# Two token streams through a fp32 transformer step: at each normalisation, four weight pieces used stream by stream on both sides

## The chip, the cores and the metric

The kernel runs on one core of one Trainium2 chip. The metric is the device time of one execution in microseconds (us); lower is better. The core has a matrix engine (PE, called TensorE) with its own weight loads (PEld), a vector engine (DVE), a scalar engine (ACT), a general engine (POOL) and a queue engine (SP) that issues most of the transfers. Each takes its own instructions strictly in the order of the program; they wait for one another through semaphores.

## The reference, cut to what matters

Two streams of 128 tokens by 2048 channels (context tokens, stream 0; latent tokens, stream 1) go through two layers with the same weights, in float32:

```python
h = rms_norm(x, norm_mix_pre[l]) * (1 + cm) + sm           # cm, sm, gm, cf, sf, gf: modulation vectors
mix = attention_and_gmlp(h @ w_in[l])                      # w_in 2048 x 4608
x = x + gm * rms_norm(mix @ w_out[l], norm_mix_post[l])    # w_out 2048 x 2048
h = rms_norm(x, norm_ffn_pre[l]) * (1 + cf) + sf
f = (silu(h @ w_gate[l]) * (h @ w_up[l])) @ w_down[l]      # 5632 hidden channels
x = x + gf * rms_norm(f, norm_ffn_post[l])
```

The modulation vectors are `silu(cond) @ mod_w[l] + mod_b[l]`, six vectors of 2048 for each layer and stream. So between two weight matrices there stands twice in each layer the same bridge: square sums of the last product, a first reciprocal root, the new x, square sums of x, a second reciprocal root, the normalised x, its transposition, its scale and shift. Here each such bridge is called an edge. Edge 0 lies between w_out and w_gate of layer 0, edge 1 between w_down of layer 0 and w_in of layer 1, edge 2 is edge 0 of layer 1, and edge 3 is the end (only the first half of a bridge, then the output).

## The kernel before, in words

**Weights.** Every weight matrix is read in pieces of 256 rows by 512 columns (512 KB, `KB = 2` blocks of 128 rows). A float32 product is made of three products of shorter numbers: ACT copies a piece to a rounded form (`whi`, L1038), DVE subtracts to get the rest (`wlo`, L1268); this is `split`. For each block of 128 rows and each stream, `products` (L739) issues three matmuls, each with its own weight load: x low by whi, x high by wlo, x high by whi. One piece is thus 12 matmuls (2 blocks, 2 streams, 3 products), one unit of 8 pieces (`UNIT`) is 96 matmuls and fills 128 x 512 results of both streams, in the banks A0 and A1, or B0 and B1. `raw`, `whi` and `wlo` are rings of four pieces (`RING`), and ACT and DVE split four pieces ahead of PE (`LEAD`): piece j+4 can only be split when PE has used piece j (`w_used`). The transfer of a piece waits until its place in `raw` has been split (`lo_ready`).

**Order at an edge.** `dense` (L707) runs a unit, both streams in each piece. After the last unit of w_out or w_down ACT and DVE read the banks to `f`, square (`square`, L1052), gate (`gated`, L1437) and make the mean (`mean_square`, L1313), POOL raises it to the power -1/2 (`power`, L617), DVE makes the new x (`post`, L1427), ACT squares that, POOL makes the second root, DVE multiplies (`normal_chunks`, L1343), PE turns blocks of 4 x 128 columns of one stream (`turn_x`, L829), DVE and ACT scale and shift them (`pre_part`, L1353 and L1088), ACT rounds them (`high`, L1056) and DVE takes the rest (`low`, L1322). All of this is done for both streams at once, with one wait for both. PE may begin the next unit when the first block of both streams has passed (`xt_ready`); the second block comes at row block 4, and the turns of blocks 2 and 3 stand between the matmuls at row blocks 1 and 3. Two of the four pieces that lie ahead are split at the edge by ACT at once and by DVE one in each pause (`left_over`, `LEFT = 2`); the two others are split before it.

**Modulation.** The products for the modulation vectors are put between the pieces in bursts of four pieces of `mod_w` (`mod`, L801, 16 matmuls of 32 columns of weights); they have a ring of four pieces of their own (`mraw`). In the units of w_out there are four bursts, one after piece 3 of each unit, and two more follow behind the last unit, before the turns of edge 0 or 2, with the read-out of the finished vector (`mod_tail`: ACT L1067, PE L821, DVE `mod_cols`). Other vectors are made by DVE in the pieces of w_gate, w_up and w_down (`accumulate`, L1290), from the ninth piece after edge 0 and 2 on. At edge 1 nothing of them lies on PE before the first unit; w_in has a burst after piece 3 of a unit.

## Time and profile before

| | |
|---|---|
| time, median of 3 runs | 2475.52 us (2470.42 to 2483.92) |
| profiled execution, its own time | 2475.68 us |
| its span, first to last instruction | 2473.9 us |
| PE busy | 2323.5 us (94%), mean granted clock 0.97 |
| DVE busy, ACT busy, POOL busy | 1507.5 us (61%), 984.0 us (40%), 65.9 us (3%) |
| moved by DMA | 609.94 MB, mean 247 GB/s |

The span is what the trace covers; the profiled execution's own time holds 1.8 us more. PE's clock has two levels here, 2.4 GHz (granted clock 1.00) and 1.2 GHz (0.50).

### The profile page before, as it was taken

The numbers are of one execution on the slowest core, as the hardware profiler recorded it, in microseconds if no ns is written. First come the engines' busy times: TensorE is split into PE (matmuls) and PEld (weight loads), VectorE is DVE, ScalarE is ACT, GpSimd is POOL, SyncE is SP. The second block draws the span as 40 slices with busy tenths as digits, with TensorE's granted clock in tenths as the row PEclk, the third lists the DMA queues.
The fourth block names the chain that finished last, engine by engine and source line by source line (L and its number), as shares of the span: only waits on it lengthen the run. The fifth ranks groups of instructions, "written<-read, shape, count | busy, mean of one in ns | idle before, by whom it ended". The sixth has DMA issues, their size and how long they took to land.

```text
span 2473.9 us, 28233 instructions
## 1 busy us (share of the span) xinstructions
PE 2323.5 (94%) x10892; PEld 1810.9 (73%) x10892; DVE 1507.5 (61%) x1637; ACT 984.0 (40%) x1253; POOL 65.9 (3%) x90
## 2 busy tenths in 40 slices
PE   5999978989999999999979998798999999999997
PEld 2776646768888887888757775475888888878886
DVE  2555453568886788688765444545788644454455
ACT  2333242454444443334444333345444444434443
POOL 1001020000000000000000101000000000000000
PEclk8999989989999999999989999998999999999999
DMA  8779887758777777787746876776777666556664
GB/s 298 272 286 340 324 285 288 256 203 269 267 257 246 272 262 248 236 271 266 269 166 221 300 264 219 273 278 225 260 268 258 219 194 191 188 183 195 189 220 137
DMA packets 269318, 609.94 MB, mean 247 GB/s; under 512 B 19116, under 2 KB 19296, under 8 KB 267840
## 3 DMA queue, kind: packets, MB, share of 16 engines
q1 hardware_dynamic: 264832, 589.37, 70.0%
q0 software_dynamic: 4352, 18.76, 2.0%
q8 instruction: 87, 1.43, 0.2%
q14 instruction: 47, 0.39, 0.0%
HBM read 603.79 MB, written 5.45 MB: 246 GB/s over the span
## 4 chain that ended last, share of the span: by engine, by line
PE 85%; DMA 6%; issue 4%; DVE 2%; ACT 1%; SPq 1%; POOL 0%; POOLq 0%; DVEq 0%; ACTq 0%
PE bank_A L743 39%; PE bank_B L743 37%; DMA mraw<-in_mod_w 6%; PE bank_M L801 3%; PE bank_X L829 2%; PE bank_M L790 1%; PE bank_T L821 1%; DVE wlo L1268 0%; ACT xtmp L1088 0%; PE bank_M L733 0%; ACT junk L1052 0%; PE bank_B L915 0%; SPq L464 0%; ACT whi L1038 0%; DVE f L1343 0%
## 5 line engine op out<-in xcount | busy, mean ns | idle before, releaser
L1268 DVE TENSOR_TENSOR wlo<-raw,whi 128x1024 fp32r<-128x1024 f32 x736 | 898.9, 1224 | 794.5 <-ACT whi L1038 794.3
L1038 ACT CAST whi<-raw 128x1024 fp32r<-128x1024 f32 x736 | 770.2, 1049 | 1231.1 <-PE bank_A L743 622.5
L743 PE MATMUL bank_A<-whi,xt_lo 128*128 128x512 f32 x1136 | 450.3, 396 | 6.4 <-DVE xt_lo L1322 5.9
L743 PE MATMUL bank_A<-wlo,xt_hi 128*128 128x512 f32 x1136 | 446.1, 393 | 0.0
L743 PE MATMUL bank_A<-whi,xt_hi 128*128 128x512 f32 x1136 | 445.7, 392 | 0.0
L743 PE MATMUL bank_B<-whi,xt_lo 128*128 128x512 f32 x1104 | 433.6, 393 | 0.5 <-issue 0.5
L743 PE MATMUL bank_B<-wlo,xt_hi 128*128 128x512 f32 x1104 | 430.0, 390 | 0.0
L743 PE MATMUL bank_B<-whi,xt_hi 128*128 128x512 f32 x1104 | 429.8, 389 | 0.0
L1290 DVE SCALAR_TENSOR_TENSOR acc<-mraw,cond,acc 128x1024 f32<-128x1024 f32 x240 | 297.1, 1279 | 0.0
L743 PEld LDWEIGHTS bank_A<-whi,xt_lo 128*128 128x128 f32 x1136 | 215.8, 190 | 71.0 <-issue 25.0
L743 PEld LDWEIGHTS bank_B<-whi,xt_lo 128*128 128x128 f32 x1104 | 207.2, 188 | 58.3 <-issue 15.1
L743 PEld LDWEIGHTS bank_A<-whi,xt_hi 128*128 128x128 f32 x1136 | 215.4, 190 | 45.6
L743 PEld LDWEIGHTS bank_A<-wlo,xt_hi 128*128 128x128 f32 x1136 | 215.8, 190 | 43.7
L743 PEld LDWEIGHTS bank_B<-whi,xt_hi 128*128 128x128 f32 x1104 | 207.2, 188 | 43.5
L743 PEld LDWEIGHTS bank_B<-wlo,xt_hi 128*128 128x128 f32 x1104 | 207.4, 188 | 41.8
L801 PE MATMUL bank_M<-mraw,cond 128*32 128x512 f32 x768 | 109.8, 674 | 42.9 <-DMA mraw<-in_mod_w 42.8
L743 PE MATMUL bank_A<-whi,ht_lo 128*128 128x512 f32 x352 | 138.9, 394 | 0.0
L743 PE MATMUL bank_A<-wlo,ht_hi 128*128 128x512 f32 x352 | 137.7, 391 | 0.0
L743 PE MATMUL bank_A<-whi,ht_hi 128*128 128x512 f32 x352 | 137.5, 391 | 0.0
L743 PE MATMUL bank_B<-whi,ht_lo 128*128 128x512 f32 x352 | 137.3, 390 | 0.0
L743 PE MATMUL bank_B<-wlo,ht_hi 128*128 128x512 f32 x352 | 137.0, 389 | 0.0
L743 PE MATMUL bank_B<-whi,ht_hi 128*128 128x512 f32 x352 | 136.9, 389 | 0.0
(190 smaller groups left out, 1429.7 us busy)
## 6 DMA issues: line engine op xcount, KB each, us to landing
mraw<-in_mod_w SPq DMA_DIRECT2D x384, 512.0 KB, 5.7
raw<-in_w_gate SPq DMA_DIRECT2D x176, 512.0 KB, 3.7
raw<-in_w_up SPq DMA_DIRECT2D x176, 512.0 KB, 4.2
raw<-in_w_down SPq DMA_DIRECT2D x176, 512.0 KB, 4.6
raw<-in_w_in SPq DMA_DIRECT2D x144, 512.0 KB, 6.0
raw<-in_w_out SPq DMA_DIRECT2D x64, 512.0 KB, 5.1
gate_mix<-gate_rows POOLq DMA_DIRECT2D x4, 1024.0 KB, 6.5
gate_ffn<-gate_rows POOLq DMA_DIRECT2D x4, 1024.0 KB, 9.5
```

What stands on the lines that cost most here:

```text
L743: mm = pe.matmul(bank[f"{pair}{s}"][:], xs[:, k, t], ws_[:, slot, kb, :], start=(k == first and n == 0), stop=(k == (nk - 1 if last is Non ...
L790: mm = pe.matmul(bank["M"][g:g + 32, :], cond[:, 2 * k:2 * k + 32], mraw[:, j % RING, kb, :], start=(k < 4), stop=(k >= KD - 4))
L801: mm = pe.matmul(bank["M"][32 * c:32 * c + 32, :], cond[:, 2 * k:2 * k + 32], mraw[:, ring_piece(m, j + c // 2) % RING, c % 2, :], start=( ...
L821: mm = pe.matmul(bank["T"][:, w * t:w * t + w], mrow[:, t * P:(t + 1) * P], sel[:], start=True, stop=True)
L829: mm = pe.transpose(bank[b][:, n * P:(n + 1) * P], t, ident[:])
L1038: act.copy(whi[:, ph % RING], raw[:, ph % RING]).then_inc(hi_ready, 1)
L1268: dve.tensor_tensor(wlo[:, ph % RING], raw[:, ph % RING], whi[:, ph % RING].bitcast(F32), ALU.subtract).then_inc(lo_ready, 1)
L1290: ins = dve.scalar_tensor_tensor(out=acc[:, h, s, :], in0=w, scalar=c, in1=acc[:, h, s, :], op0=ALU.mult, op1=ALU.add)
```

## The change

On both sides of an edge four pieces (`APART`) are no longer used by both streams in each piece. PE runs stream 0 through all four, reports `half_done`, and then runs stream 1 through the same four; `w_used` is raised in stream 1's pass. The edge's work is split by stream and written out by hand as one `turnover` on ACT and one on DVE, POOL gets four powers at an edge in place of two, and the eight turns of blocks get an order of their own (`turn_order`, `TURN_AT`): stream 0's blocks 0 and 1 before its pass of four pieces, stream 1's blocks 0 and 1 within that pass, the other four in stream 1's pass and at piece 4. All four pieces ahead are now split within `turnover`. In w_out the bursts for the modulation stand after pieces 3, 8, 13, 19 and 24 of its 32 pieces (`OUT_MODS`), one stays behind the end; the transfers of all six are issued between the pieces (`OUT_FETCH`). At the end the output of stream 0 is issued first. The changed places, shortened:

```diff
+APART = 4
+
+def turn_order(l, which):
+    if l == which == 0:
+        return [(s, b) for b in range(ND) for s in range(2)]
+    return [(0, 0), (0, 1), (1, 0), (1, 1), (0, 2), (1, 2), (0, 3), (1, 3)]
+
+TURN_AT = {((0,), 5): (2, 3), ((1,), 1): (4,), ((1,), 3): (5,), ((1,), 6): (6,), ((0, 1), 8): (7,)}
+
+def scaled_by_act(l, which, i):
+    return i % 2 == 1 if l == which == 0 else i in (0, 2, 5, 7)
...
+OUT_MODS = {3: (0, range(0, 4)), 8: (0, range(4, 8)), 13: (1, range(0, 4)), 19: (1, range(4, 8)), 24: (2, range(0, 4))}
+OUT_FETCH = {4: (0, (0, 1)), 5: (0, (2, 3)), 11: (0, (4, 5)), 12: (0, (6, 7)), 16: (1, (0, 1)), 17: (1, (2, 3)),
+             22: (1, (4, 5)), 23: (1, (6, 7)), 27: (2, (0, 1)), 28: (2, (2, 3)), 31: (2, (4, 5, 6, 7))}
...
-                both(u + 1, w, CH, m, l, LOAD_SECOND)
-                for i in range(1, ND // 2):
-                    both(i * 2 + u, w, i * 2 * CH, i + m, l, LOAD_FIRST)
-                    both(i * 2 + (u + 1), w, i * 2 * CH + CH, i + m, l, LOAD_SECOND)
+                for q in range(LEAD, ND * UNIT):
+                    i, j = divmod(q, UNIT)
+                    both(u + i, w, i * CH, js=[j])
+                    if q in OUT_FETCH:
+                        mi, js = OUT_FETCH[q]
+                        mod_chunk(m + mi, l, js)
                 first_unit(plan.at[(l, "up", 0)][0], a["w_gate"][l], 0)
-                mod_chunk(m + MOD_OUT, l)
                 for g, (c0, n) in enumerate(GROUPS):
                     u, _, _ = plan.at[(l, "up", g)]
...
                     first_unit(plan.at[(l + 1, "win")][0], a["w_in"][l + 1], 0)
             sp.wait_ge(kv_stored, 16 * 4 * DEPTH)
-            for n in range(ND):
-                for s in range(2):
+            for s in range(2):
+                for n in range(ND):
                     c = slice(n * CH, (n + 1) * CH)
-                    sp.wait_ge(x_new, 16 * DEPTH - 8 + 2 * n + s + 1)
+                    sp.wait_ge(x_new, 16 * DEPTH - 8 + ND * s + n + 1)
...
+            def edge_powers(l, which):
+                k = 1 + 4 * edge_of(l, which)
+                if last_edge(l, which):
+                    for s in range(2):
+                        power(ms[:, s:s + 1], rstd[:, s:s + 1], ms_ready, k + s + 1, rstd_ready)
+                    return
+                for s in (0, 0, 1, 1):
+                    k += 1
+                    power(ms[:, s:s + 1], rstd[:, s:s + 1], ms_ready, k, rstd_ready)
+            power(ms[:], rstd[:], ms_ready, 1, rstd_ready)
...
-            def dense(u, pair, i, hi, lo, nk=KD, ph=0, ready=None, m=None, behind={}):
+            def dense(u, pair, i, hi, lo, nk=KD, ph=0, ready=None, m=None, behind={}, first=0, last=0):
 
 
 
                 free(pair + "0", i)
                 free(pair + "1", i)
-                for j in range(nk // KB):
-                    pe.wait_ge(lo_ready, u * UNIT + (ph + j + 1))
-                    slot = (ph + j) % RING
-                    for kb in range(KB):
-                        k = j * KB + kb
-                        if ready:
-                            ready(k)
-                        mm = products(pair, k, hi, lo, slot, kb, nk)
-                    mm.then_inc(w_used, 1)
-                    if j in behind:
-                        mod(m, behind[j])
-                    dve_vector(u * UNIT + ph + j)
+                n = nk // KB
+                for js in (range(first), range(first, n - last), range(n - last, n)):
+                    together = js.start == first and js.stop == n - last
+                    for streams in [(0, 1)] if together else [(0,), (1,)]:
+                        for j in js:
+                            if streams[0] == 0:
+                                pe.wait_ge(lo_ready, u * UNIT + (ph + j + 1))
+                            slot = (ph + j) % RING
+                            for kb in range(KB):
+                                k = j * KB + kb
+                                if ready:
+                                    ready(k, streams)
+                                mm = products(pair, k, hi, lo, slot, kb, nk, streams=streams)
+                            if streams[-1] == 0:
+                                if j == n - 1:
+                                    mm.then_inc(half_done, 1)
+                                continue
+                            mm.then_inc(w_used, 1)
+                            if j in behind:
+                                mod(m, behind[j])
...
-            def turn_x(l, which, b):
-                for s, (bk, i) in enumerate(plan.at[(l, "pre_uses", which)][b]):
-                    pe.wait_ge(xn_ready, 8 * (2 * l + which) + 2 * b + s + 1)
-                    turn(bk, i, [f[:, s, (4 * b + t) * P:(4 * b + t + 1) * P] for t in range(4)])
+            def turn_x(l, which, i):
+                s, b = turn_order(l, which)[i]
+                pe.wait_ge(xn_ready, 8 * edge_of(l, which) + i + 1)
+                turn(*plan.at[(l, "pre_uses", which)][i], [f[:, s, (4 * b + t) * P:(4 * b + t + 1) * P] for t in range(4)])
 
             def pre(l, which):
 
 
-                def ready(k):
-                    if k in (1, 3):
-                        turn_x(l, which, 2 + k // 2)
+                done = xt_count(l, which) - 8
+                def ready(k, streams):
+                    if (streams, k) in TURN_AT:
+                        for i in TURN_AT[(streams, k)]:
+                            turn_x(l, which, i)
                     if k % 4 == 0:
-                        pe.wait_ge(xt_ready, xt_count(l, which) - 8 + 2 * (k // 4 + 1))
+                        pe.wait_ge(xt_ready, done + {(0,): 1 + k // 4, (1,): 3 + k // 4, (0, 1): 2 + k // 2}[streams])
                 turn_x(l, which, 0)
                 turn_x(l, which, 1)
...
-                    mod_tail(i + m)
-                mod(m + MOD_OUT)
+                for i in range(ND):
+                    at = {q % UNIT: mj for q, mj in OUT_MODS.items() if q // UNIT == i}
+                    def burst(k, streams):
+                        if k % KB == 0 and k // KB - 1 in at:
+                            mi, js = at[k // KB - 1]
+                            mod(m + mi, js)
+                    dense(i + u, "AB"[i % 2], i // 2 + use["AB"[i % 2] + "0"], xt_hi, xt_lo, ready=burst,
+                          last=APART if i == ND - 1 else 0)
+                mod(m + MOD_OUT, range(UNIT // 2, UNIT))
                 mod_tail(m + MOD_OUT)
                 ready = pre(l, 1)
...
+            def turnover(l, which, u, ph, pieces, use, split, m=None):
+                def x_squares(s):
+                    for n in range(ND):
+                        act.wait_ge(x_new, 8 * edge_of(l, which) + ND * s + n + 1)
+                        square(x[:, s, n * CH:(n + 1) * CH], ssx[:, s, n:n + 1])
+                n = ND - 1
+                if which == 0:
+                    act.wait_ge(half_done, edge_of(l, which) + 1)
+                    act.copy(f[:, 0, n * CH:D], bank["B0"][:]).then_inc(freed["B0"], 1)
+                act.wait_ge(freed["B0"], use["B0"] + 3)
+                f_square(0, n)
+                if last_edge(l, which):
+                    act.wait_ge(freed["B1"], use["B1"] + 3)
+                    return f_square(1, n)
+                split(u, ph + pieces)
+                split(u, ph + pieces + 1)
+                x_squares(0)
+                act.wait_ge(freed["B1"], use["B1"] + 3)
+                f_square(1, n)
+                if m:
+                    mod_row(m)
+                split(u, ph + pieces + 2)
+                split(u, ph + pieces + 3)
+                l2, w2 = l + which, 1 - which
+                act.wait_ge(vec_ready, vec_count(l2, w2))
+                pre_scale(l2, w2, 0)
+                pre_high(l2, w2, 0)
+                x_squares(1)
+                pre_high(l2, w2, 1)
+                pre_scale(l2, w2, 2)
+                pre_high(l2, w2, 2)
+                pre_high(l2, w2, 3)
...
+            def turnover(l, which, u, ph, pieces, split, vectors=None):
+                now, end = edge_of(l, which), last_edge(l, which)
+                sq, rs = sq_count(l, which), 1 + 4 * now
+                c = slice((ND - 1) * CH, D)
+                def last_chunk(s):
+                    if which == s == 0:
+                        return
+                    if s == 0:
+                        dve.wait_ge(half_done, now + 1)
+                    else:
+                        dve.wait_ge(w_used, u * UNIT + ph + pieces)
+                    b = f"B{s}"
+                    if which:
+                        dve.tensor_tensor(f[:, s, c], f[:, s, c], bank[b][:], ALU.add).then_inc(freed[b], 1)
+                    else:
+                        dve.tensor_copy(f[:, s, c], bank[b][:]).then_inc(freed[b], 1)
+                def add(s):
+                    for n in range(ND):
+                        t = slice(n * CH, (n + 1) * CH)
+                        dve.scalar_tensor_tensor(out=x[:, s, t], in0=f[:, s, t], scalar=rstd[:, s:s + 1], in1=x[:, s, t],
+                                                 op0=ALU.mult, op1=ALU.add).then_inc(x_new, 1)
+                last_chunk(0)
+                gated(l, which, ND - 1, 0, sq + 7)
+                mean_square(ssq, sq + 7, slice(0, 1))
+                if vectors:
+                    vectors(0)
+                dve.wait_ge(rstd_ready, rs + 1)
+                add(0)
+                last_chunk(1)
+                if end:
+                    gated(l, which, ND - 1, 1, sq + 8)
+                    mean_square(ssq, sq + 8, slice(1, 2))
+                    dve.wait_ge(rstd_ready, rs + 2)
+                    return add(1)
+                split(u, ph + pieces)
+                mean_square(ssx, sq + 11, slice(0, 1))
+                gated(l, which, ND - 1, 1, sq + 12)
+                mean_square(ssq, sq + 12, slice(1, 2))
+                l2, w2 = l + which, 1 - which
+                dve.wait_ge(rstd_ready, rs + 2)
+                normal(l2, w2, 0, 1)
+                if vectors:
+                    vectors(1)
+                dve.wait_ge(vec_ready, vec_count(l2, w2))
+                dve.wait_ge(rstd_ready, rs + 3)
+                add(1)
+                pre_low(l2, w2, 0)
+                split(u, ph + pieces + 1)
+                pre_scale(l2, w2, 1)
+                mean_square(ssx, sq + 16, slice(1, 2))
+                pre_low(l2, w2, 1)
+                dve.wait_ge(rstd_ready, rs + 4)
+                normal(l2, w2, 2, 3)
+                split(u, ph + pieces + 2)
+                pre_scale(l2, w2, 3)
+                split(u, ph + pieces + 3)
+                pre_low(l2, w2, 2)
+                pre_low(l2, w2, 3)
+                normal(l2, w2, 4, 5, 6, 7)
```

## Rows read from the trace of the kernel before

**Rows 1.** The page, chain that ended last, by engine.

```profile
PE 85%; DMA 6%; issue 4%; DVE 2%; ACT 1%; SPq 1%; POOL 0%; POOLq 0%; DVEq 0%; ACTq 0%
```

**Rows 2.** Windows (length; PE, PEld, DVE, ACT, POOL busy; PEclk; DMA share; GB/s).

```profile
406.67:503.89 97.22, 97.22 (x456) 74.47 (x456) 42.45 (x39) 36.92 (x45) 0.00 (x0) 0.98 0.79 277
498.45:552.66 54.21, 44.39 (x193) 32.15 (x193) 35.99 (x64) 28.52 (x56) 2.33 (x2) 0.78 0.56 196
1271.59:1326.81 55.22, 38.37 (x169) 29.46 (x169) 35.92 (x63) 27.44 (x54) 2.31 (x2) 0.78 0.47 160
1694.76:1747.21 52.45, 42.05 (x193) 30.41 (x193) 35.91 (x64) 28.77 (x56) 2.33 (x2) 0.84 0.54 195
```

**Rows 3.** Timeline of PE at edge 0: start, us, what, idle before.

```profile
503.50 0.39 PE L743 MATMUL bank_B<-whi,xt_hi 128*128 128x512 f32 x1
...
515.57 1.87 PE L821 MATMUL bank_T<-rsel,mrow 128*128 128x8 f32 x8 [0.72 <-ACT mrow L1067]
...
524.25 0.77 PE L743 MATMUL bank_A<-whi,xt_lo 128*128 128x512 f32 x1 [0.75 <-DVE xt_lo L1322]
524.82 0.63 PE L743 MATMUL bank_A<-wlo,xt_hi 128*128 128x512 f32 x1
525.24 0.63 PE L743 MATMUL bank_A<-whi,xt_hi 128*128 128x512 f32 x1
...
533.93 1.03 PE L829 MATMUL bank_X<-ident,f 128*128 128x128 f32 x8
```

**Rows 4.** Timeline of DVE at edge 0.

```profile
505.30 1.51 DVE L1437 TENSOR_TENSOR f<-f,gate_mix 128x512 f32<-128x512 f32 x2 [0.68 <-ACT junk L1052]
...
507.12 1.23 DVE L1268 TENSOR_TENSOR wlo<-raw,whi 128x1024 fp32r<-128x1024 f32 x1
508.96 5.39 DVE L1427 SCALAR_TENSOR_TENSOR x<-f,rstd,x 128x512 f32<-128x512 f32 x8 [0.61 <-POOL rstd L617]
...
518.16 1.67 DVE L1343 TENSOR_SCALAR f<-x,rstd 128x512 f32<-128x512 f32 x4
519.93 1.36 DVE L1353 TENSOR_SCALAR xtmp<-bank_X,scal,shift 128x128 f32<-128x128 f32 x4
522.81 1.29 DVE L1322 TENSOR_TENSOR xt_lo<-xtmp,xt_hi 128x512 fp32r<-128x512 f32 x2 [1.52 <-ACT xt_hi L1056]
```

**Rows 5.** Timeline of ACT at edge 0.

```profile
509.74 0.63 ACT L1052 ACTIVATE junk<-x 128x512 f32<-128x512 f32 x1 [1.78 <-DVE x L1427]
...
510.56 0.63 ACT L1052 ACTIVATE junk<-x 128x512 f32<-128x512 f32 x1
```

**Rows 6.** Timeline of POOL, edge 0 and edge 3.

```profile
507.29 1.63 POOL L617 TENSOR_TENSOR rstd<-ms,minus_half 128x2 f32<-128x2 f32 x1 [115.00 <-DVE ms L1314]
...
2464.40 0.71 POOL L617 TENSOR_TENSOR rstd<-ms,minus_half 128x2 f32<-128x2 f32 x1 [68.61 <-DVE ms L1314]
```

**Rows 7.** Chain in order of time: the unit after edge 0's first.

```profile
552.66 21.76 PE bank_B L743 x96
```

**Rows 8.** Timeline of PE: the burst in w_out's last unit.

```profile
490.50 0.39 PE L743 MATMUL bank_B<-whi,xt_hi 128*128 128x512 f32 x1
...
492.67 0.50 PE L743 MATMUL bank_B<-whi,xt_lo 128*128 128x512 f32 x1
```

**Rows 9.** Timeline of PE: edge 1's first turn, edge 3's last matmul.

```profile
1291.26 1.97 PE L829 MATMUL bank_X<-ident,f 128*128 128x128 f32 x8 [14.23 <-DVE f L1343]
...
2460.38 0.39 PE L743 MATMUL bank_B<-whi,ht_hi 128*128 128x512 f32 x1
```

**Rows 10.** Timeline of DVE at edge 3.

```profile
2462.41 1.51 DVE L1437 TENSOR_TENSOR f<-f,gate_ffn 128x512 f32<-128x512 f32 x2 [0.24 <-ACT junk L1052]
2463.95 0.16 DVE L1313 TENSOR_REDUCE msum<-ssq 128x2 f32<-128x8 f32 x1
...
2465.14 5.39 DVE L1427 SCALAR_TENSOR_TENSOR x<-f,rstd,x 128x512 f32<-128x512 f32 x8 [0.83 <-POOL rstd L617]
```

**Rows 11.** Busy time by window: w_in of layer 0, most DMA.

```profile
206.00:230.00 24.00, 24.00 (x129) 17.38 (x128) 11.97 (x14) 6.77 (x7) 0.00 (x0) 1.00 0.95 355
```

More of the change, by code:

```diff
@@ L1101, in start, with pre_late @@
+            def pre_late(l, which, j):
+                if j < 2:
+                    pre_pair(l, which, 4 + 2 * j)
             def start():
```

254 lines of the change are left out of this document (123 added, 131 removed).

## The prediction

> **What bounds the kernel now.** I read the chain that ended last first, since it says which engine's work sets the end: PE has 85% of it [rows 1]. Then the busy time by window, to see where PE is not full. In w_out of layer 0 it is busy for 97.22 of 97.22 us [rows 2]. In the windows around the norms it is busy for 44.39 of 54.21, 38.37 of 55.22 and 42.05 of 52.45 us, with a mean granted clock of 0.78 to 0.84, so even part of the busy time there is at half speed [rows 2]. I set these windows to begin 5.44 us before the last matmul's end (four pieces of one stream: 24 matmuls of 21.76 / 96 = 0.227 us each [rows 7]) and to end with the first unit behind the edge. The zero of all times below is that beginning.
>
> The timeline says what PE waits for. At edge 0 the last matmul ends at 503.89, the first one of w_gate starts at 524.25, 20.4 us later, behind DVE's xt_lo [rows 3]. Between them lies one long chain over DVE, ACT and POOL that works on both streams before it hands anything on: eight adds take 5.39 us, ACT's squares of x follow at 0.82 us each [rows 4, 5]. Edge 1 has 14.23 us without any PE work before its first turn [rows 9], edge 3 ends in the same chain's first half [rows 10]. The dense units themselves (21.76 us) the change leaves as they are: the same matmuls, the same pieces, so it can win only at the four edges. A perfect cover is bounded by these windows: 54.2 - 5.4 - 21.8 = 27.0 us for edge 0, of which turns and bursts need some 7.
>
> **The first matmul behind edge 0, after the change.** Stream 0 ends at 0, stream 1's pass covers PE until 5.4. DVE can gate stream 0 at 1.4, as it does now after both (503.89 to 505.30 [rows 3, 4]). One gate 0.7 (half of the two), then mean, root and hand-over 1.2, from edge 3, where nothing stands beside POOL (2463.95 to 2465.14 [rows 10]): the add starts at 3.3. Four adds, half of 5.39 [rows 4], to 6.0. DVE's copy of B1 0.7 and one split 1.2 [rows 4] to 7.9. ACT's squares begin 0.8 behind the add and take 0.82 each [rows 5]: 4.1 to 7.4, the last square of f to 8.2. DVE: mean 0.36, gate 0.7, mean 0.36, to 9.4 (POOL begins 0.45 behind a mean's start, 2463.95 to 2464.40 [rows 6, 10]; I count 0.36 on DVE); two normalised chunks at 0.42 (1.67 for four [rows 4]) to 10.3. Meanwhile the finished modulation vector: ACT's copy behind its squares to 8.8, PE's turn 1.87 [rows 3] to 10.8, DVE's four small instructions for the vectors, each like a mean's 0.16 with its hand-over [rows 10], to 11.5. Four adds for stream 1, 2.7, one low 0.65 (half of 1.29 [rows 4]): PE starts at 14.9. Before it was 524.25 - 498.45 = 25.8. That is 10.9 us earlier, but not yet the gain.
>
> **What is late next.** The weights. Formerly two pieces were split before the edge and two in its pauses; now all four can be split only as stream 1's pass frees them, and on DVE three of them stand behind the new x of stream 1. Between PE's start and piece 2 DVE has a split 1.2, a scale 1.36, a mean 0.36, a low 0.65, two normalised chunks 0.84, a split 1.2 [rows 4]: 5.6 us and about 0.4 of waits, so piece 2 is there at 21.0, where 12 matmuls of stream 0 take 2.7 us at full clock and 5.1 at half. Then the two turns of stream 1 (0.52 each at full clock: 1.03 for two [rows 3]), at half clock double, and behind them on DVE a scale 1.36 and the last split 1.2: piece 3 at 25.3. Its six matmuls end at 26.6. Stream 1's pass takes 5.4 and has three turns, 1.6, and one wait for a bank, 0.6: 34.2. A turn 0.5, four pieces for both streams 10.9, one late split 0.6: the unit ends at 46.2, before at 54.2. Edge 0 wins 8.0.
>
> **Waits that are new, and what queues behind them.** ACT waits for half_done with the last pieces' splits already behind it; what follows is the whole turnover, and nothing of it could start earlier. DVE's wait for the modulation vector (0.4 us by the chain above: it would be free at 10.3 and PE's turn ends at 10.8) holds the adds of stream 1, the split of piece 1 and thereby PE. ACT's copy of that vector stands behind eight squares, so each 0.1 us more there goes through to PE. SP has no new kind of wait, but the last four mod_w transfers are issued at piece 31 and need the burst after piece 24; behind them are the four first pieces of w_gate, which PE wants only at 14.9, over 20 us later. Those cost nothing.
>
> **Edge 2** is the same chain, but before it took only 52.45 (the clock rose earlier): 6.3. **Edge 1** has no modulation vector to wait for, has an add in place of the copy on the path (0.2 more), and one burst in its unit before and after: start at 14.3, end at 46.9 against 55.2: 8.3. **Edge 3:** gate at 1.6, as 2460.77 to 2462.41 [rows 9, 10], 0.7, 1.2, adds to 6.2; stream 1's last chunk 0.7, square 0.8, gate 0.7, mean and root 1.2, adds 2.7: 12.5 with hand-overs. The adds now end at 2470.53, which is 15.2: it wins 2.7, and the output transfers behind them stay as long.
>
> **The bursts.** Of the two that stood behind w_out's end, one is now before stream 0's last pass. There it costs 492.67 - 490.50 less one matmul, 1.94 us [rows 8], in each layer: before, both lay in the chain's shadow. That is -1.9 at edges 0 and 2. The two powers more at an edge lie on POOL, whose queue holds nothing else there. The weights of stream 0 and 1 in another order are the same number of weight loads and matmuls: nothing. The start of layer 0 keeps its order: nothing.
>
> **Sum.** 8.0 - 1.9 + 8.3 + 6.3 - 1.9 + 2.7 = 21.5 us. I take 3.0 off, 1 us for each of three edges, for the clock. The mean of 0.78 says that some 24 us of the windows of edges 0 and 1 ran at half speed, 0.84 some 17 us at edge 2 [rows 2]; my chain counts half speed only from PE's first wait to 20. Bounds of this term: nothing, or 4.4 us an edge, if it stays at 1.2 GHz until 32 (some 18 matmuls more and six turns; one matmul takes 0.43, 524.82 to 525.24, instead of 0.227 [rows 3, 7]). The profiled execution took 2475.68 us, 1.8 more than its span and 0.2 from the median: 2475.7 - 18.5 = 2457.
>
> **POOL beside DVE.** The first root took 1.63 us at edge 0, beside a split of 1.23 that began 0.17 earlier, and 0.71 at edge 3 beside nothing [rows 4, 6]. In the new order nothing follows the first mean on DVE, so I take 0.71; the second to fourth have a gate, a normalised chunk or a low beside them. If all were like the slow one it would be 3 x 0.9 more for an edge, 8 us in all. The Trainium skill (SBUF — State Buffer, "Who interferes with whom") says that a VectorE instruction with two SBUF inputs and a GpSimd one that reads SBUF shut each other out for a whole instruction, whichever began first. By that rule the trace agrees, and the second and third root would each add up to 0.9.
>
> **Rivals.** (a) *The clock stays down.* In the new order PE has four waits (2.1, 2 to 3, 1 and 2 us) where it had long ones, and thin work between them. The price is the upper bound above: 3 x 4.4 less the 3.0 taken, 2467. The Trainium skill (TensorE: Matmul & The Clock Gate, "HAM oscillation — how this bites in real kernels") tells of waits between short bursts of matmuls that keep the clock at half rate; by it this would be the likelier case, while the trace has the next unit at 21.76 us, full speed [rows 7]. (b) *DVE is the bound, so the split stays late.* If pieces 4 and 5 come 3 us late as well (DVE has 2 x (1.2 + 1.36 + 1.3) = 7.7 us of work for them, with its waits 9.8, covered by 10.9), 9 us of the gain go: 2466. (c) *The wait only changes its name:* every hand-over between the four engines is a place for some tenths more; 30 of them an edge at 0.2 us are 6, for three edges the whole 18: 2475. (d) *Better:* the clock never falls at edges 0 and 2 and no split is late: 3 + 3 x 2 more, 2448. (e) *Slower:* the bursts' transfers. From piece 4 to 31 of w_out there are now 28 + 24 transfers of 0.524 MB, 27.3 MB, in 27 x 2.72 + 5 x 1.94 = 83 us: 328 GB/s, where the window moved 277 [rows 2]. For it: that is 18% more than the stage ever had. Against: w_in moved 355 GB/s for 24 us with PE busy throughout [rows 11]. Were 277 all that this mix of rows gets, the stage would take 98.6 us, 15.5 more in each layer: 2457 + 31 = 2488. It decides the sign below 27.3 MB / 92.3 us = 296 GB/s.
>
> **How the numbers follow.** The sum, 2451 to 2463: 0.50. Better: 0.10. (a) and (b) together, 2463 to 2471: 0.22. (c): 0.10. (e): 0.08. Half a per cent, 12.4 us, is about what a measurement of this kernel can tell from no change: the limits are 2463.1 and 2487.9. Faster: 0.50 + 0.10 and a little of (a), 0.63; same: the rest of (a) and (b), 0.19, (c), and 0.03 of (e), whose price lies on the limit, 0.32; slower 0.05. The range leaves out (c), (e) and the far end of (d): 2448 to 2471.
>
> **What would show it.** Right: at edges 0 and 2 the first matmul on w_gate starts 9 to 11 us nearer to the end of w_out's last one (20.4 now, 9 to 10 then), PE then waits for wlo of pieces 2 and 3 and not for xt_lo, and w_out takes 2 us more. The last adds end in two groups of four. Wrong: waits of PE for mraw or of ACT for raw within w_out (e); a granted clock of 0.5 until the second unit (a); DVE without a pause of over 0.5 us until the ninth piece, and waits for wlo behind piece 4 (b).

## The result, and the profile after

The changed kernel takes 2453.68 us (median of 5 runs, 2450.63 to 2467.93) against 2475.52 (median of 5 as well); the ratio is 0.9925, 95% interval 0.9898 to 0.9952. Predicted were 2457.0 us, 2448 to 2471; the time lies below the 2463.1 from which the prediction calls a kernel faster. Its profiled execution has the highest time of the five (2467.93 us), only 7.8 us below the one of before (2475.68). A second measurement of the same kernel below (2457.73, ratio 0.9924) has a profiled execution near its median.

The page of the changed kernel, the chain that ended last, then PE's rows of the grouped instructions; before it was 85% PE, 6% DMA and 4% issue [rows 1]. PE's idle time ahead of the group shown was 6.4 us before and is 20.8 now: before, PE waited earlier, ahead of the turns ([rows 9]), now it waits for the operand itself.

```profile
PE 87%; DMA 5%; DVE 4%; ACT 2%; issue 1%; POOL 0%; SPq 0%; DVEq 0%; POOLq 0%; ACTq 0%
...
L793 PE MATMUL bank_A<-whi,xt_lo 128*128 128x512 f32 x1136 | 455.0, 401 | 20.8 <-DVE xt_lo L1419 12.8
```

Busy time by window: w_out of layer 0 up to the zero of edge 0 only (the first window of [rows 2] goes on to the last matmul's end, 5.44 us more; without them it was 91.78), its first 10 us and its last 33, then edges 0, 1 and 2 from their zero to the first matmul of the second unit behind them, as in [rows 2]:

```profile
408.84:503.07 94.23, 94.23 (x445) 70.85 (x442) 39.99 (x37) 34.81 (x43) 0.00 (x0) 0.98 0.87 300
408.84:418.84 10.00, 10.00 (x40) 8.17 (x37) 2.45 (x2) 2.10 (x2) 0.00 (x0) 0.81 0.97 346
...
470.00:503.07 33.07, 33.07 (x161) 24.58 (x160) 14.15 (x13) 11.30 (x15) 0.00 (x0) 1.00 0.92 327
...
503.07:549.72 46.65, 38.88 (x177) 29.41 (x176) 36.06 (x68) 29.73 (x57) 2.76 (x4) 0.89 0.40 123
1271.61:1319.92 48.31, 38.37 (x170) 29.03 (x169) 35.51 (x63) 28.61 (x55) 2.40 (x4) 0.86 0.52 166
1694.37:1741.07 46.70, 38.90 (x178) 29.40 (x176) 36.15 (x68) 29.74 (x57) 2.76 (x4) 0.89 0.39 125
```

At edge 0 PE is busy for 38.9 us instead of 44.4, since one of the two bursts has gone to w_out and more of the matmuls run at full clock, and idle for 7.8 instead of 9.8; both parts make the window shorter. Edge 1 shows another split: as many busy microseconds as before (38.4), but 9.9 idle for 16.9. In w_out PE has no idle time, and the last 33 us, with the transfers of the added pieces in them, move 327 GB/s.

Timeline of PE at edge 0 (zero 503.07), its main waits, and where its clock changed:

```profile
508.44 1.92 PE L853 MATMUL bank_M<-mraw,cond 128*32 128x512 f32 x16
511.54 1.06 PE L873 MATMUL bank_T<-rsel,mrow 128*128 128x8 f32 x8 [1.17 <-ACT mrow L1126]
512.72 1.09 PE L881 MATMUL bank_X<-ident,f 128*128 128x128 f32 x8
517.24 0.77 PE L793 MATMUL bank_A<-whi,xt_lo 128*128 128x512 f32 x1 [3.43 <-DVE xt_lo L1419]
...
522.87 0.50 PE L793 MATMUL bank_A<-whi,xt_lo 128*128 128x512 f32 x1 [0.49 <-DVE wlo L1368]
527.30 0.50 PE L793 MATMUL bank_A<-whi,xt_lo 128*128 128x512 f32 x1 [1.90 <-DVE wlo L1368]
...
528.88 0.63 PE L793 MATMUL bank_A<-whi,xt_lo 128*128 128x512 f32 x1
...
532.21 0.39 PE L793 MATMUL bank_A<-whi,xt_lo 128*128 128x512 f32 x1
```

The first matmul stands at 14.2 (25.8 before, [rows 3]). The next two waits are for `wlo`, the split weights of pieces 2 and 3. A matmul's duration of 0.63 instead of 0.39 is the mark of the lower clock. It stands in the matmuls from 517.24 to 521.6, and it comes back once, from 528.88 until 531.9, behind the 1.90 us of waiting. I call that the second fall.

Timeline of DVE at edge 0, what answers to [rows 4], and POOL, which answers to [rows 6]:

```profile
504.49 0.69 DVE L1593 TENSOR_TENSOR f<-f,gate_mix 128x512 f32<-128x512 f32 x1 [4.46 <-ACT junk L1111]
...
506.24 2.74 DVE L1481 SCALAR_TENSOR_TENSOR x<-f,rstd,x 128x512 f32<-128x512 f32 x4 [0.68 <-POOL rstd L651]
508.90 0.69 DVE L1476 COPY f<-bank_B 128x512 f32<-128x512 f32 x1
509.50 1.22 DVE L1368 TENSOR_TENSOR wlo<-raw,whi 128x1024 fp32r<-128x1024 f32 x1
...
512.98 0.18 DVE L1409 COPY modt<-bank_T 128x32 f32<-128x32 f32 x1
...
513.75 2.74 DVE L1481 SCALAR_TENSOR_TENSOR x<-f,rstd,x 128x512 f32<-128x512 f32 x4
516.41 0.69 DVE L1419 TENSOR_TENSOR xt_lo<-xtmp,xt_hi 128x512 fp32r<-128x512 f32 x1
...
521.60 1.22 DVE L1368 TENSOR_TENSOR wlo<-raw,whi 128x1024 fp32r<-128x1024 f32 x1
524.75 1.37 DVE L1449 TENSOR_SCALAR xtmp<-bank_X,scal,shift 128x128 f32<-128x128 f32 x4 [1.93 <-PE bank_X L881]
526.03 1.22 DVE L1368 TENSOR_TENSOR wlo<-raw,whi 128x1024 fp32r<-128x1024 f32 x1
```

```profile
505.64 0.56 POOL L651 TENSOR_TENSOR rstd<-ms,minus_half 128x1 f32<-128x1 f32 x1 [110.36 <-DVE ms L1414]
```

Here the last wait explains itself: DVE stands still for 1.93 us until PE has turned stream 1's block, with piece 3's split, which could have run (ACT had made its `whi` by 513.4), queued behind that scale. PE then waits 1.90 us for just this split.

The last adds, at edge 3 (zero 2451.18), come in two groups of four and end at 11.9; they ended at 15.2 before [rows 10]:

```profile
2454.52 2.74 DVE L1481 SCALAR_TENSOR_TENSOR x<-f,rstd,x 128x512 f32<-128x512 f32 x4 [0.68 <-POOL rstd L651]
...
2460.39 2.74 DVE L1481 SCALAR_TENSOR_TENSOR x<-f,rstd,x 128x512 f32<-128x512 f32 x4 [0.67 <-POOL rstd L651]
```

**All edges and kernels on one scale.** I read these from the timelines, in us behind each edge's zero (5.44 before the last matmul's end). "Unit end" is the first matmul of the second unit; for before that is 0.16 less than in [rows 2], which went by the chain. w_out is from its first matmul to the zero.

| kernel | edge 0: first matmul / unit end | edge 1 | edge 2 | edge 3: span's end | w_out, layer 0 / 1 |
|---|---|---|---|---|---|
| before | 25.80 / 54.05 | 25.22 / 55.06 | 26.03 / 52.29 | 18.57 | 91.78 / 90.38 |
| changed | 14.17 / 46.65 | 14.12 / 48.31 | 14.17 / 46.70 | 14.92 | 94.23 / 94.26 |
| changed, again | 14.15 / 45.04 | 14.11 / 46.68 | 14.15 / 46.69 | 14.92 | 92.50 / 93.92 |
| bursts only | 25.28 / 54.09 | 25.22 / 55.36 | 25.28 / 51.52 | 18.54 | 93.30 / 93.82 |
| bursts as before | 23.48 / 55.96 | 14.11 / 48.29 | 23.20 / 54.08 | 14.90 | 92.47 / 90.38 |
| apart ahead only | 23.59 / 49.65 | 23.54 / 50.87 | 23.75 / 49.00 | 14.92 | 94.73 / 92.50 |
| apart behind only | 20.08 / 50.96 | 19.55 / 53.70 | 20.07 / 50.97 | 20.33 | 94.42 / 92.50 |
| split beside the root | 15.06 / 47.59 | 15.06 / 47.63 | 15.05 / 47.51 | 14.93 | 94.47 / 93.78 |
| piece 3 before the scale | 14.16 / 43.88 | 14.11 / 45.49 | 14.16 / 43.84 | 14.93 | 93.15 / 92.52 |
| piece 2 earlier too | 14.16 / 42.68 | 14.12 / 44.59 | 14.16 / 43.44 | 14.89 | 93.43 / 92.72 |

**Where the time came from.** From the profiled execution of before to that of the changed kernel the edges give 7.4 + 6.8 + 5.6 + 3.7 = 23.4 us, w_out takes 2.4 + 3.9 = 6.3 back: 17.1. The spans differ by 7.8 only. The other 9.3 lie in stretches between the edges, whose code the diff leaves as it is nearly everywhere: 2.2 ahead of w_out of layer 0 (whose beginning scatters from 403.1 to 410.7 us over the executions here), 2.8 from the end of edge 0's unit to edge 1, 2.5 in w_in and the attention of layer 1, 1.8 behind edge 2. The second measurement's execution does not show the last three (+0.5, -0.6 and +0.4 us), so I take them for the profiled execution's own. In that second execution the edges give 26.6, w_out takes 4.3 back, w_out of layer 0 begins 4.1 later and the rest loses 0.2: 18.1, as its span (2455.8) has it.

### The profile page after: what moved, and what is told of

Read it like the earlier page. It is cut to its first block, busy times and chain, and to the rows that moved or that the text cites. A ratio compares the mean times of both kernels' runs of the same rounds, so it can differ in the third digit from the quotient of the medians.

```text
span 2466.1 us, 28259 instructions
## 1 busy us (share of the span) xinstructions
PE 2332.2 (95%) x10892; PEld 1816.3 (74%) x10892; DVE 1507.0 (61%) x1651; ACT 984.2 (40%) x1253; POOL 67.5 (3%) x97
## 4 chain that ended last, share of the span: by engine, by line
PE 87%; DMA 5%; DVE 4%; ACT 2%; issue 1%; POOL 0%; SPq 0%; DVEq 0%; POOLq 0%; ACTq 0%
PE bank_A L793 40%; PE bank_B L793 38%; DMA mraw<-in_mod_w 5%; PE bank_M L853 3%; PE bank_X L881 2%; PE bank_M L842 1%; DVE wlo L1368 1%; DVE x L1481 0%; PE bank_T L873 0%; ACT whi L1097 0%; DVE xtmp L1449 0%; PE bank_M L783 0%; PE bank_B L970 0%; ACT junk L1111 0%; PE bank_A L970 0%
## 5 line engine op out<-in xcount | busy, mean ns | idle before, releaser
L793 PE MATMUL bank_A<-whi,xt_lo 128*128 128x512 f32 x1136 | 455.0, 401 | 20.8 <-DVE xt_lo L1419 12.8
```

The lines of the kernel that those rows point to most:

```text
L793: mm = pe.matmul(bank[f"{pair}{s}"][:], xs[:, k, t], ws_[:, slot, kb, :], start=(k == first and n == 0), stop=(k == (nk - 1 if last is Non ...
```

## The experiments

The kernels were timed in two groups of four, on two chips, each group with its own runs of the kernel before (medians 2475.50 and 2475.11 us, 23 runs each). The changed kernel again, bursts only, bursts as before and piece 3 before the scale are the first group; across the groups, times are compared by the ratios.

**The same kernel again, and its halves: the bursts.** The first is the changed kernel unaltered.

> The changed kernel once more, with a profile, since its profiled execution (2467.93 us) was the slowest of five (median 2453.68). Theory (the gain is made in the four edges): the windows from stream 0's end to the first unit's end are 46.8, 48.5 and 46.8 us again within 0.5, whatever the whole time is, and the end takes 14.9; the spread of 17 us lies in the attention and at the start, where PE waits for mod_w. Rival (the edges themselves vary by several us from run to run, by the clock): an edge differs by over 2 us from the first trace.

It took 2457.73 us (2455.52 to 2458.87), ratio 0.9924 (0.9911 to 0.9937): the gain is 19 us with a narrower interval. Neither expectation holds: edges 0 and 1 end 1.6 us earlier each and edge 2 as before, which is more than 0.5 and less than 2. Of the 10.3 us between the two profiled spans 3.2 lie there, 2.1 in w_out and 6.9 in the stretches between; the start is 1.9 longer in the second. The clock did not fall a second time at edge 0 here (nor at edge 1), though the wait for piece 3 was again 1.90:

```profile
517.38 0.77 PE L793 MATMUL bank_A<-whi,xt_lo 128*128 128x512 f32 x1 [2.55 <-DVE xt_lo L1419]
523.01 0.50 PE L793 MATMUL bank_A<-whi,xt_lo 128*128 128x512 f32 x1 [0.17 <-DVE wlo L1368]
...
527.44 0.50 PE L793 MATMUL bank_A<-whi,xt_lo 128*128 128x512 f32 x1 [1.90 <-DVE wlo L1368]
529.62 0.60 PE L881 MATMUL bank_X<-ident,f 128*128 128x128 f32 x4
```

The kept traces price the second fall. From the first matmul to the unit's end there are 32.5 us with it and 30.9 without it at edges 0 and 2, and 34.2 and 32.6 at edge 1: 1.6 us each time. Over the five profiled executions in which PE waits 1.89 or 1.90 us for piece 3 (changed, again, bursts as before, apart behind only, split beside the root) it came at 9 of 15 edges. How long the first stretch at the lower clock lasts changes nothing: it ends 2.7 to 5.6 us behind the first matmul, and those times stay, since PE then waits for piece 2 or 3 anyway.

Two kernels then part the bursts from the reordering. "Bursts only" is the kernel before with the changed kernel's places for bursts and their transfers; "bursts as before" is the changed kernel with the old ones:

```diff
# bursts as before (from the changed kernel)
-                for q in range(LEAD, ND * UNIT):
-                    ...
-                    if q in OUT_FETCH:
+                both_rest(u, w, 0, m, l)
+                both(u + 1, w, CH, m, l, LOAD_SECOND)
...
                 first_unit(plan.at[(l, "up", 0)][0], a["w_gate"][l], 0)
+                mod_chunk(m + MOD_OUT, l)
...
-                    dense(i + u, ..., ready=burst, last=...)
-                mod(m + MOD_OUT, range(UNIT // 2, UNIT))
+                    dense(i + u, ..., m=i // 2 + m, behind=IN_SECOND if i % 2 else IN_FIRST, last=...)
+                mod(m + MOD_OUT)
```

> The kernel before with the new places of the modulation bursts and their transfers in w_out alone; the edges as before. Theory: w_out 1.94 us longer in each layer; at the edge the second burst no longer waits for its transfer, but the norm chain ends later anyway (T turn at 515.57 and the normalised chunk at 518.16 in the kernel before), so nothing comes back: 2475.5 + 3.9 = 2479 us. Rival (the transfers are too dense, 328 GB/s): waits of PE for mraw or of ACT for raw in w_out, 10 to 30 us more. Second rival (the burst's waits were on the path of the edge): 2475 or less.

> The changed kernel with the bursts of w_out where they were before: two stand behind the last unit again, the second with its transfer issued only there. Theory: at edges 0 and 2 the finished vector is now what the new chain waits for: second burst done some 16.7 us after stream 0's end, first matmul on w_gate at 23 instead of 14.1, 9 us more for each of two edges, less 1.94 in w_out: 2454 + 14 = 2468 us; edge 1 unchanged at 48.5. Rival (the norm chain on DVE and ACT is what counts and hides the bursts): 2454 - 3.9 = 2450.

Bursts only: 2483.16 us (2472.89 to 2486.86), ratio 1.0018 (1.0005 to 1.0031), a small loss; the ratio gives 4.5 us, the two medians 7.7. The two w_out's are 1.5 and 3.4 us longer, and the first matmul comes only 0.5 and 0.75 earlier, since the vector alone was not what held PE there. Bursts as before: 2468.93 us (2461.91 to 2476.57), ratio 0.997 (0.9956 to 0.9984). Edge 1, which has no vector on its way, keeps its 14.11; at edges 0 and 2 PE starts at 23.5 and 23.2, and the units there end 1.9 and 1.8 us later than in the kernel before. All that this kernel gains it gains at edges 1 and 3. Timelines of PE and of DVE at edge 0 of that kernel say why:

```profile
510.72 1.93 PE L853 MATMUL bank_M<-mraw,cond 128*32 128x512 f32 x8 [4.38 <-DMA mraw<-in_mod_w]
513.69 1.93 PE L853 MATMUL bank_M<-mraw,cond 128*32 128x512 f32 x8 [1.04 <-DMA mraw<-in_mod_w]
516.35 1.88 PE L873 MATMUL bank_T<-rsel,mrow 128*128 128x8 f32 x8 [0.72 <-ACT mrow L1120]
522.53 0.77 PE L793 MATMUL bank_A<-whi,xt_lo 128*128 128x512 f32 x1 [2.51 <-DVE xt_lo L1413]
```

```profile
518.26 0.19 DVE L1403 COPY modt<-bank_T 128x32 f32<-128x32 f32 x1 [9.23 <-PE bank_T L873]
```

The modulation weights land late, the vector is turned at 17.3 behind the zero instead of 8.5, and DVE stands still for 9.23 us until it has it. The scale of stream 0's block needs the vector itself; stream 1's adds, which the hand-written order puts behind it, add little: DVE ends them 0.3 us after ACT has rounded stream 0's block. So the moved bursts lose 4.5 us alone (0.18%) and are worth 11 (2468.93 - 2457.73) together with the new order.

**The two halves of the reordering.**

```diff
# apart ahead only
-TURN_AT = {((0,), 5): (2, 3), ((1,), 1): (4,), ((1,), 3): (5,), ((1,), 6): (6,), ((0, 1), 8): (7,)}
+TURN_AT = {((0, 1), 0): (2, 3), ((0, 1), 1): (4,), ((0, 1), 3): (5,), ((0, 1), 6): (6,), ((0, 1), 8): (7,)}
...
-                          first=APART if ready else 0)
# apart behind only
-                          last=APART if i == ND - 1 else 0)
...
-                        dve.wait_ge(half_done, now + 1)
+                        dve.wait_ge(w_used, u * UNIT + ph + pieces)
```

> The changed kernel, but only the last four pieces ahead of an edge are used by stream; the first unit behind it takes both streams together again, so PE needs stream 1's first block as well before its first matmul (its turns 2 and 3 go before piece 0). Theory (each half of the reordering gives PE 5.4 us of work on one side of the same chain, and the two lean on each other: the chain begins early because of the one, and PE can use the early stream 0 only because of the other): stream 0's adds still start at 3.3 behind the zero of the edge, but the first matmul only when stream 1's low part is there, at about 21 to 22.5, where the changed kernel has 14.2 and the kernel before 25.8; the unit ends at 49.5 to 51, not at 45 to 46.7; edge 3 keeps its 3.7. That is 3.5 us of gain at each of three edges and 3.7 at the last, less some 3 for the bursts: 2465 to 2469. Rival 1 (the gain is only the earlier start, the order behind the edge does nothing): 2457, as the changed kernel. Rival 2 (each half alone gives half): 2466 here and 2466 with the other half alone.

> The other half alone: both streams end together ahead of the edge, so stream 0's last chunk is complete only 5.44 us behind the zero; behind the edge the four pieces are used by stream, as in the changed kernel. Theory: the whole chain stands 5 us later: stream 0's adds start at 8.7 instead of 3.3, the first matmul comes at 19 to 19.6 instead of 14.2, the unit ends at 51 to 52 instead of 46.7, and edge 3 loses its 3.7 us and perhaps 1 more, since its adds come in two groups that nothing covers. Sum: 3 x 5 + 4 = 19 more than the changed kernel, 2474 to 2478, so next to nothing is left of the gain although half of the reordering is there. Rival 2 (each half alone gives half): 2466.

Ahead only: 2470.32 us (2463.17 to 2478.38), ratio 0.9979 (0.9964 to 0.9994). Behind only: 2477.46 (2473.34 to 2486.18), ratio 1.0009 (0.9999 to 1.0019), nothing. The unit ends are near those of the theory (49.0 to 50.9, and 51.0 to 53.7, of which edge 1's is 1.7 beyond it); the first matmul comes at 23.5 to 23.8 with the first kernel, 1 us and more beyond my 22.5, and at 19.6 to 20.1 with the second, up to 0.5 beyond. With the order ahead alone PE waits for stream 1's block; with the order behind alone the whole chain stands 5.4 to 5.9 later, and edge 3 ends 1.8 later than in the kernel before. PE's first turn and first matmul at edge 0, ahead only (zero 498.09):

```profile
516.55 1.94 PE L881 MATMUL bank_X<-ident,f 128*128 128x128 f32 x8 [7.72 <-DVE f L1434]
...
521.68 0.80 PE L793 MATMUL bank_A<-whi,xt_lo 128*128 128x512 f32 x1 [3.19 <-DVE xt_lo L1418]
```

Both rivals fall: it is not the earlier start alone, and neither half alone brings half of the time (5 us and -2 us by the medians, both together 18). But each of these three numbers has the cost of the moved bursts in it. At the edges alone, from the table, the order ahead gives 15.5 us, the order behind 4.0, both together 23.4 and 26.6 in the two executions. So the order ahead is the larger part, and what the two give only together is 4 to 7 us, with the second falls of 1.6 us in these numbers. What the edge's work split by stream gives without either order, no run tests.

**The root beside a split.**

```diff
                 if vectors:
                     vectors(0)
+                if not end:
+                    split(u, ph + pieces)
                 dve.wait_ge(rstd_ready, rs + 1)
                 add(0)
                 last_chunk(1)
...
-                split(u, ph + pieces)
```

> The changed kernel, but at the three inner edges DVE makes the first split of the next weights before it waits for the first root, where the kernel before had one, and no longer behind stream 0's adds. Theory (the root on POOL is drawn out by a split that runs beside it): the root takes 1.6 us as in the kernel before (1.63) and not the 0.56 of the changed kernel; stream 0's adds begin 1.1 later; of these 0.6 reach the first matmul, since the squares of x on ACT are what DVE's mean waits for and the split no longer stands before it: first matmul at 14.7 to 14.9 against 14.2, time 2457.7 + 3 x 0.6 = 2459.5. Rival (the 1.63 of the kernel before came from something else, the root takes 0.6 beside the split too): the adds begin 0.6 later, for the split itself, first matmul 14.2 to 14.4, time 2458.

Timelines of DVE and of POOL of that kernel at edge 0 (zero 499.65):

```profile
502.19 1.23 DVE L1368 TENSOR_TENSOR wlo<-raw,whi 128x1024 fp32r<-128x1024 f32 x1
503.87 2.74 DVE L1481 SCALAR_TENSOR_TENSOR x<-f,rstd,x 128x512 f32<-128x512 f32 x4 [0.46 <-POOL rstd L651]
```

```profile
502.22 1.62 POOL L651 TENSOR_TENSOR rstd<-ms,minus_half 128x1 f32<-128x1 f32 x1 [111.76 <-DVE ms L1414]
508.28 0.55 POOL L651 TENSOR_TENSOR rstd<-ms,minus_half 128x1 f32<-128x1 f32 x1 [4.44 <-DVE ms L1414]
```

The root is back at 1.62 (0.56 in the changed kernel), the adds begin at 4.2 instead of 3.2, and the first matmul at 15.06 instead of 14.17, 0.9 later where I expected 0.6. The time is 2460.98 us (2453.78 to 2467.1), ratio 0.9942 (0.9926 to 0.9958). The intervals of 0.9924 and 0.9942 touch, so that loss is shown by the first matmul at the three edges (0.9 each time), not by the time.

**The late weights.** The changed kernel has on DVE, behind stream 1's normalised chunks, the split of piece 2, the scale of stream 1's block, the split of piece 3. The scale waits for PE. Two kernels move splits ahead:

```diff
# piece 3 before the scale
                 split(u, ph + pieces + 2)
-                pre_scale(l2, w2, 3)
                 split(u, ph + pieces + 3)
+                pre_scale(l2, w2, 3)
# piece 2 earlier too
                 mean_square(ssx, sq + 16, slice(1, 2))
+                split(u, ph + pieces + 2)
                 pre_low(l2, w2, 1)
                 dve.wait_ge(rstd_ready, rs + 4)
                 normal(l2, w2, 2, 3)
-                split(u, ph + pieces + 2)
```

> The changed kernel with one exchange on DVE: the split of the fourth piece stands ahead of the scale of turn 3, in the 1.93 us in which DVE waits for that turn. Theory (the late weights are what is left of the edge): PE's wait of 1.90 us for wlo before piece 3 goes at each of three edges, and with it the fall of the clock behind it (0.43 for a matmul at 528.9 to 531.9, some 2 us): 2 to 4 us an edge, 2454 - 9 = 2445 to 2448 us. Rival (stream 1's inputs are next, the gain is lost again at once): PE waits for xt_lo before stream 1's pass, under 1 us an edge, 2452.

> As the kernel that splits piece 3 before it scales stream 1's second block (2449.96), and DVE splits piece 2 as well before the low part of stream 0's second block, 1.2 us earlier. Theory (with the splits of pieces 2 and 3 in time, what is left of the wait is stream 1's operand, whose chain the moved split delays by 0.4 to 0.8): the wait for wlo at piece 2, 1.1 us, goes and the one for xt_lo ahead of stream 1's pass grows from 0.5 to about 2; unit end 43.9 to 44.5, time 2450 to 2452, no gain. Rival (late weights are all that is left): 3 x 1.1 us less, unit end 42.8, time 2446.7.

The first took 2449.96 us (2447.5 to 2453.2), ratio 0.9898 (0.988 to 0.9915), where I expected 2445 to 2448. Its interval touches that of the changed kernel (0.9911 to 0.9937); the edges are clearer. Its unit ends come 1.2, 1.2 and 2.9 us before those of the changed kernel's second execution, and 2.8 to 2.9 before those of the first: 1.2 is the shorter wait (1.90 gone, 0.47 for `xt_lo` come in its place), 1.6 the second fall, which came at none of the six edges of these two kernels. The second took 2447.75 (2445.54 to 2449.41), ratio 0.9889 (0.9876 to 0.9902), the best of all, 1.2, 0.9 and 0.4 us before the first at the edges. PE at edge 0 in the first (zero 500.24) and in the second (zero 499.90):

```profile
520.02 0.50 PE L793 MATMUL bank_A<-whi,xt_lo 128*128 128x512 f32 x1 [1.11 <-DVE wlo L1368]
...
520.83 1.04 PE L881 MATMUL bank_X<-ident,f 128*128 128x128 f32 x8
...
524.40 0.50 PE L793 MATMUL bank_A<-whi,xt_lo 128*128 128x512 f32 x1 [0.47 <-DVE xt_lo L1419]
```

```profile
519.29 1.04 PE L881 MATMUL bank_X<-ident,f 128*128 128x128 f32 x8
522.86 0.51 PE L793 MATMUL bank_A<-whi,xt_lo 128*128 128x512 f32 x1 [0.45 <-DVE xt_lo L1419]
```

My theory for the second, that stream 1's operand would be the limit and nothing be gained, is wrong at the edges; the rival had the unit end at 42.8, and edge 0 has 42.68. The operand is no chain of its own: it begins with PE's turns of stream 1's blocks, and these stand in PE's queue behind piece 2. With piece 2 in time the turns come at 19.4 instead of 20.6, and the operand comes 1.2 us earlier too (23.0 for 24.2), so the wait for it stays 0.45. The times (intervals 0.988 to 0.9915 and 0.9876 to 0.9902) don't tell the two kernels apart by themselves.

## Why the prediction was right, step by step

| step | predicted | measured, changed kernel / again |
|---|---|---|
| edge 0: adds start / end | 3.3 / 6.0 | 3.2 / 5.9 |
| edge 0: first matmul | 14.9 | 14.2 / 14.2 |
| edge 0: piece 2, piece 3 ready | 21.0, 25.3 | 19.8, 24.2 / 19.8, 24.2 |
| edge 0: unit end without the clock term | 46.2 | 46.65 / 45.04 |
| edge 1: first matmul, unit end | 14.3, 46.9 | 14.1, 48.31 / 14.1, 46.68 |
| edge 2: gain | 6.3 | 5.6 / 5.6 |
| edge 3: gain | 2.7 | 3.65 / 3.65 |
| bursts, each layer | -1.9 | -2.4 and -3.9 / -0.7 and -3.5 |
| clock term, three edges | -3.0 | -4.8 / -1.6 (second falls, 1.6 each) |
| sum less the clock term | 18.5 | 17.1 / 22.4 in the stages; 0.75% (0.5 to 1.0) of the time, 18.6 |

**The chain ahead of the first matmul** was right link by link, 0.7 us too long. The vector came a little earlier than I took: its turn ran at full clock (1.06 us where I had 1.87 from [rows 3]); PE comes to it from a burst and 1.17 us of waiting, before it came from waits of 4.42, 0.82 and 0.72 us. So my wait of DVE for the vector (0.4) does not exist: at 512.98 DVE goes on without a stop. The distance from w_out's last matmul to w_gate's first is 8.7 us, just under the 9 to 10 that the prediction named as its sign.

**What is late next** was named rightly: PE's waits for `wlo` of pieces 2 and 3. The two kernels with the earlier splits show that this is a cost and not only a label: 6 and 9 us by the ratios.

**The clock term.** I took 3.0 off for three edges. Against the chain without it the unit ends lie 0.45, 1.4 and 0.55 us beyond (edge 2 against 52.45 - 6.3), 2.4 in all, in the first execution and 0.8 below it in the second. That is a net of two things. The second fall cost 1.6 us where it came: at all three edges of the first execution, 4.8, and at one of the second, 1.6. The rest of the chain was 2.4 too long in the prediction, the first matmul, taken up to 0.7 too late, among it. So 1 us for each edge is near the mean of the 15 places above (9 x 1.6 / 15), but no row had given it. The Trainium skill (TensorE: Matmul & The Clock Gate, "HAM oscillation — how this bites in real kernels") tells of waits between bursts of matmuls that send the clock down. By that section the trace agrees ahead of the first matmul, where PE waits 1.17 and 3.43 us between small pieces of work and the matmuls behind take 0.63. For the second fall there are only the rows: behind the same 1.90 us of waiting it came in some executions and not in others. Rival (a) had the clock low until 32 at each edge; in the changed kernel's two executions it was back by 19.8, and after a second fall by 28.9.

**The sum** was met more closely than its terms. The chain was 2.4 us too long at three edges and edge 3 gave 0.95 more; the bursts cost 2.5 more than taken in the first execution and 0.4 in the second; the second falls cost 4.8 and 1.6 where 3.0 were taken. The stages then give 17.1 and 22.4. That the ratio gives 18.6 where 18.5 was forecast is in part luck; the mechanism and the order of size are not.

**The bursts.** 1.94 was a good price for one burst: where w_out ran at full clock throughout, it took 92.50 in place of 90.38, 2.1 more. The rest of 3.9 is the lower clock in the first 10 us of the stage (0.81 in both layers of the first execution), which I had not counted, and which the kernel before shows too in its layer 0 (91.78). What the prediction missed is the other side of the step: it counted the bursts as a cost and took the early vector for granted in the chain. Without them the first matmul at edges 0 and 2 stays at 23, and nothing is won there.

**Edge 3** gave 0.95 more: the adds ended at 11.9 and not at 12.5, and the output behind them takes 0.4 less.

**POOL.** I took 0.71 for the undisturbed root and 0.56 came. The second root, where I feared up to 0.9 more, takes 1.10 at edges 0 and 2 and 0.54 at edge 1; the third takes 0.55, 0.75 and 0.55. At edge 0 this cost nothing: the second root ends at 512.15, and DVE works on its two means until 512.11. That a split was to blame for 1.63 is shown by putting one back (1.62).

**The rivals.** (b) is half true: pieces 2 and 3 were late, pieces 4 and on were not. (c), 0.2 us for each hand-over, would have shown in the first matmul; it came earlier than summed. (d) came by half at edges 0 and 1 of the second execution: no second fall, unit end 45.04 at edge 0, but the first matmuls still ran at 0.63 and piece 3 was still 1.90 us late; with the late splits removed as well it is 42.68. (e) is refuted: w_out moved 300 GB/s on average, above the 296 from which it would have decided the sign, and 327 in its last third, while PE was busy for 94.23 of 94.23 us. The longest wait for `mraw` in w_out over the kernels with the moved bursts is 1.1 us, once (split beside the root, layer 1). The kernel with the moved bursts alone loses 0.2%, not 1.3%.

What stays open is why the first profiled execution is slower outside the edges. The windows between them, in the first and in the second execution, behind edge 0 and then behind edge 1, say this much:

```profile
549.72:1271.61 721.89, 715.91 (x3212) 587.97 (x3211) 564.03 (x517) 297.94 (x321) 1.63 (x3) 0.99 0.78 257
1319.92:1600.11 280.19, 251.35 (x1315) 183.62 (x1313) 131.06 (x162) 99.29 (x147) 22.30 (x27) 0.96 0.77 267
```

```profile
548.27:1267.84 719.57, 713.59 (x3212) 586.09 (x3211) 563.49 (x517) 297.80 (x321) 1.63 (x3) 1.00 0.76 257
1314.52:1591.60 277.08, 249.92 (x1315) 182.81 (x1313) 131.33 (x162) 99.18 (x147) 22.17 (x27) 0.97 0.76 270
```

For the same number of matmuls PE is busy 2.3 and 1.4 us longer, at a granted clock lower by 0.01, and 1.5 us longer behind edge 2; that is 5.2 of the 6.9 us between the two executions in these stretches. What sent the clock down there no run shows.

## What to carry to other kernels

When a chain between two matrix products works on two independent streams, use the last weight pieces before it and the first ones behind it stream by stream: each half alone gave 5 us or nothing, both gave 18 to 22. And it needs everything else on the chain moved early enough: with the vector from another product left where it was, two of the three inner edges lost what they should have won. In a hand-written order, look for an instruction that waits with one behind it that could run: exchanging a scale and a split gave another 0.26% (ratio 0.9924 to 0.9898, some 6 us). Cost each link of the chain from the rows, then ask what stands in front of it in its queue; the operand that seemed to be the next limit moved with the wait before it.

## What the runs showed of the hardware

A root on POOL of 128x1 takes 0.56 us, but 1.62 us with a DVE split (128x1024, two inputs) that began 0.03 us before it; in the kernel with piece 2 earlier the fourth root takes 1.48 beside a split that began 0.15 us before. The split itself keeps its 1.23. The same shows in the changed kernel at edges 0 and 2, where DVE's gate (128x512, two inputs) begins 0.01 us before the second root. The lengthened roots end 0.4 us behind the end of the DVE instruction, as if they had waited for it. Timelines of POOL and DVE, changed kernel, edge 0 and then edge 1:

```profile
511.05 1.10 POOL L651 TENSOR_TENSOR rstd<-ms,minus_half 128x1 f32<-128x1 f32 x1 [4.84 <-DVE ms L1414]
...
1279.69 0.54 POOL L651 TENSOR_TENSOR rstd<-ms,minus_half 128x1 f32<-128x1 f32 x1 [4.85 <-DVE ms L1414]
```

```profile
511.04 0.69 DVE L1593 TENSOR_TENSOR f<-f,gate_mix 128x512 f32<-128x512 f32 x1
...
1279.98 0.69 DVE L1593 TENSOR_TENSOR f<-f,gate_ffn 128x512 f32<-128x512 f32 x1 [0.36 <-ACT junk L1111]
```

At edge 1 the gate begins 0.29 us after the second root, and neither is lengthened. So it is with `low` (two inputs) and the fourth root at all three edges: it begins 0.30 to 0.35 us after the root, root 0.55, `low` 0.69.

The Trainium skill (SBUF — State Buffer, "Who interferes with whom") has either engine shut the other out, whichever began first. With DVE first the trace agrees (1.62, 1.48 and 1.10); with POOL first, in these four places, nothing is drawn out, and there the measurement decides.

The same program can have its clock fall in one execution and not in the next: the mean granted clock of the span was 0.971 and 0.976 in two executions of the changed kernel, and the unit behind edge 0 ended at 46.65 and at 45.04. One such fall cost 1.6 us.
